# Final sums, norm and output stores of the upper half of the tokens moved beside the last expert of a hybrid attention and expert layer

## The reference

```python
x = x + gt1 * (merged @ lp['w_out'])
h2 = rms_norm(x, lp['norm2_g']) * (1 + sc2) + sh2
x = x + gt2 * hierarchical_moe(h2, ...)      # each token: two of 16 experts, 1024 -> 256 -> 1024
...
hid = jax.nn.silu(jnp.einsum('td,edf->tef', x, w_g)) * jnp.einsum('td,edf->tef', x, w_u)
hid = hid * gate[:, :, None]
y = jnp.einsum('tef,efd->td', hid, w_d)
...
y = rms_norm(x, final_norm_g)
```

## Time and profile before

| | us |
|---|---|
| median of 3 runs | 1568.53 |
| lowest and highest of them | 1565.21 and 2982.1 |
| the profiled execution, its own time | 1567.61 |
| its span, first to last instruction | 1565.7 |

### The profile page before, as it was taken

One profiled execution on the slowest core, in us unless ns is written; L12 is line 12 of the kernel. 1 busy time (PEld: TensorE's weight loads), 2 busy tenths in 40 slices (PEclk: granted clock), 3 DMA queues, 4 the chain that ended last, 5 costly groups with the idle time before them and its releaser, 6 DMA issues.

```text
span 1565.7 us, 21878 instructions
## 1 busy us (share of the span) xinstructions
PE 1476.5 (94%) x8155; PEld 1232.6 (79%) x8155; DVE 1006.5 (64%) x1498; ACT 655.4 (42%) x890; POOL 269.0 (17%) x167
## 2 busy tenths in 40 slices
PE   5999999999999899999999999999999599999990
PEld 4788888777888678888788888888888589888880
DVE  7698433046546477778877764334556888888875
ACT  6312222221123566666566642111332367677753
POOL 0112211123324101001100000000000124444430
PEclk9999999999999999999999999999999699999995
DMA  9345443320001010000000034423524378988858
GB/s 374 136 158 184 160 162 145 109 106 28 28 31 65 34 45 0 0 0 34 12 1 0 15 104 142 150 89 116 184 82 188 111 239 264 259 270 262 254 149 290
DMA packets 52449, 194.81 MB, mean 124 GB/s; under 512 B 9370, under 2 KB 18442, under 8 KB 40992
## 3 DMA queue, kind: packets, MB, share of 16 engines
q1 hardware_dynamic: 42144, 172.31, 30.2%
q0 software_dynamic: 10240, 21.61, 6.9%
HBM read 157.03 MB, written 43.58 MB: 128 GB/s over the span
## 4 chain that ended last, share of the span: by engine, by line
PE 48%; DVE 8%; ACT 3%; DMA 3%; issue 2%; POOL 0%; DVEq 0%; SPq 0%; POOLq 0%; ACTq 0%
PE psum L1636 9%; PE psum L1816 6%; PE psum L1837 5%; PE psum L1592 4%; PE psum L1741 4%; PE psum L1820 3%; PE psum L1578 2%; PE psum L1575 2%; PE psum L1576 2%; PE psum L1752 2%; PE psum L1561 2%; PE psum L1563 2%; PE psum L1562 2%; ACT prob L1902 2%; PE psum L1801 1%
## 5 line engine op out<-in xcount | busy, mean ns | idle before, releaser
L353 PE MATMUL psum<-h_hi,w_hi 128*128 128x512 f32 x720 | 182.9, 362 | 2.1 <-issue 2.1
L353 PE MATMUL psum<-h_lo,w_hi 128*128 128x512 f32 x720 | 179.7, 358 | 0.0
L353 PE MATMUL psum<-h_hi,w_lo 128*128 128x512 f32 x720 | 179.3, 357 | 0.0
L2148 DVE TENSOR_TENSOR pT_lo<-psum,pT_hi 128x512 fp32r<-128x512 f32 x192 | 126.2, 686 | 55.7 <-ACT pT_hi L1908 55.7
L353 PEld LDWEIGHTS psum<-h_hi,w_hi 128*128 128x128 f32 x720 | 119.7, 188 | 28.8 <-issue 8.5
L1908 ACT CAST pT_hi<-psum 128x512 fp32r<-128x512 f32 x192 | 104.6, 589 | 84.4 <-PE psum L1592 84.4
L353 PEld LDWEIGHTS psum<-h_lo,w_hi 128*128 128x128 f32 x720 | 119.4, 188 | 21.7 <-issue 0.5
L353 PEld LDWEIGHTS psum<-h_hi,w_lo 128*128 128x128 f32 x720 | 119.4, 188 | 21.3
L714 POOL TENSOR_TENSOR w_lo<-w_raw,w_hi 128x1024 fp32r<-128x1024 f32 x30 | 76.0, 2533 | 319.9 <-ACT w_hi L555 319.9
L867 DVE SCALAR_TENSOR_TENSOR ada_junk<-adaT,cs_rows 128x1024 f32<-128x1024 f32 x64 | 84.3, 1317 | 65.7 <-DMA adaT<-in_w_adaT 62.5
L1902 ACT ACTIVATE prob<-psum,nmax,q_row 128x1536 f32<-128x1536 f32 x64 | 104.6, 1635 | 31.5 <-DVE nmax L2142 31.5
(11 more groups left out here) (385 smaller groups left out, 2907.8 us busy)
## 6 DMA issues: line engine op xcount, KB each, us to landing
gu_raw<-in_w_gu SPq DMA_DIRECT2D x32, 1024.0 KB, 8.5
w_raw<-in_w_in SPq DMA_DIRECT2D x16, 1024.0 KB, 5.0
adaT<-in_w_adaT SPq DMA_DIRECT2D x16, 1024.0 KB, 6.0
dn_raw<-in_w_dn SPq DMA_DIRECT2D x16, 1024.0 KB, 7.3
gates<-gst SPq DMA_DIRECT2D x14, 640.0 KB, 3.1
xt<-in_x SPq DMA_DIRECT2D x10, 512.0 KB, 8.6
merged<-gates SPq DMA_DIRECT2D x8, 640.0 KB, 4.0
stage<-gates SPq DMA_DIRECT2D x8, 640.0 KB, 3.9
```

The costliest lines, as they stand in the source:

```text
L353: mm = pe.matmul(psum[:, par_sets[j] + g:par_sets[j] + g + w], a[j][:, k, :], b[:, k, g:g + w], start=(k == 0 and a is w_hi and b is h_hi) ...
L2148: nc.vector.tensor_tensor(pT_lo[b][g % 2][:], psum[:, TP + 512 * b:TP + 512 * b + 512], pT_hi[b][g % 2][:], ALU.subtract).then_inc(s[f"a_t ...
```

## The change

- Tiles 5 to 9 (tokens 640 and up, all latent) are loaded from y_sum as soon as the additions of the last expert but one have landed, and they are squared, normed and stored without the last expert's rows.
- The last expert's rows of those tokens are handled by themselves. POOL gathers their sums from y_sum into `late[0]` and `late[1]` (row numbers in `lat_ids`, computed in `slot_table`; the other rows of the slots get numbers out of bounds and are left out). DVE adds the last expert's `yst` rows, ACT and DVE norm them, and POOL scatters them to the output, over what the tile stores left there, when all five tile stores have landed.
- The last expert's accumulating additions now write only tokens below 640. When they have landed, SP loads tiles 0 to 4. The context tiles' gate product and sum stand behind the norm of tiles 5 to 9 and of the late rows on DVE, and the sum goes to `y` instead of `x1`.
- SP's list: load 5 to 9, store 5 and 6, wait for the last additions, load 0 to 4, store 7, 8, 9, 2, 3, 4, 0, 1. `f_all` is gone.
- In the last step, slot 1 of expert 14's down product stands ahead of the second half of `gate_up` of expert 15, and writes to PSUM at `XT_PS` instead of `Y_PS`. Its gate weights on ACT and its `y_out` on DVE are ahead of `dn_high` and `dn_low` of expert 15. The down products of expert 15 go by halves of the hidden dimension: both slots with c = 0, then both with c = 1.
- In the first unit of the short attention ACT copies both halves of the probabilities.
- The branches on `n_spare` of ACT and DVE stand at the very end; their bodies load, norm and store all ten tiles again.

The diff, cut to its core:

```diff
                     nc.scalar.copy(sprobT[z % 2][0][:], psum[:, turned_at(z, 0):turned_at(z, 0) + 512]).then_inc(s["s_out_a"], 1)
+                    if z == 0:
+                        act.wait_ge(s["s_turned"], 2)
+                        nc.scalar.copy(sprobT[0][1][:], psum[:, turned_at(0, 1):turned_at(0, 1) + 512]).then_inc(s["s_out_d"], 1)
...
                 for z in range(SHORTS):
                     if z < SHORTS - 1:
                         short_low(z + 1)
-                    short_turned(z)
+                    if z:
+                        short_turned(z)
...
+        def y_at(e, r):
+
+            if isinstance(e, int) and e == NE - 2 and r:
+                return XT_PS
+            return 0 if last_rows(e, r) else Y_PS
...
-        def total(t):
-
-            return x1[:, t, :] if t < CTX_TILES else y[t][:]
-
-        LOADED = (0, 2, 1, 3) + tuple(range(4, TILES))
-        ENDED = ((2, 4), (0, 2), (4, 7), (7, TILES))
+        LATE = NE - 1
+        late = [at(f"late{r}", [P, D], F32, RHL + (20 + 4 * r) * KB) for r in range(HOME)]
...
+
+        def late_y(r):
+
+            return yst_last if r else yst[0]
+
+        ENDED = ((HALF, 7), (7, TILES), (CTX_TILES, HALF), (0, CTX_TILES))
+        LATE_AT = 2
...
-                sp.wait_ge(s["f_all"], 1)
-                for t in LOADED:
+                sp.wait_ge(s["e_down"], 2 * LATE)
+                for r in range(HOME):
+                    sp.wait_ge(s[f"e_y_st{r}"], 16 * LATE)
+
+                def load_y(t):
                     sp.dma_start(y[t][:], io["y_sum"][t * P:(t + 1) * P, :]).then_inc(landed[t], 16)
+                for t in range(HALF, TILES):
+                    load_y(t)
                 for n, t in enumerate(ended):
+                    if n == ENDED[0][1] - ENDED[0][0]:
+                        for r in range(HOME):
+                            sp.wait_ge(s[f"e_y_st{r}"], 16 * NE)
+                        for u in range(HALF):
+                            load_y(u)
                     sp.wait_ge(s["f_normed"], n + 1)
-                    sp.dma_start(io["y"][t * P:(t + 1) * P, :], total(t)).then_inc(s["f_st"], 16)
-                sp.wait_ge(s["f_st"], 16 * TILES)
+                    sp.dma_start(io["y"][t * P:(t + 1) * P, :], y[t][:]).then_inc(s["f_st" if t < HALF else "f_lat_st"], 16)
+                sp.wait_ge(s["f_lat_st"], 16 * (TILES - HALF))
+                sp.wait_ge(s["f_st"], 16 * HALF)
...
-                add_y(NE - 1, 0)
-                add_y(NE - 1, 1)
+                for r in range(HOME):
+                    pool.wait_ge(s[f"e_y_st{r}"], 16 * LATE)
+                for r in range(HOME):
+                    pass_wait(pool)
+                    nc.gpsimd.indirect_dma_start(late[r][0:T, :], None, io["y_sum"], bass.IndirectOffsetOnAxis(lat_ids[0:T, r:r + 1], 0),
+                                                 bounds_check=TOK - 1, oob_is_err=False).then_inc(s[f"e_xg{r}"], 16)
+                for r in range(HOME):
+                    pool.wait_ge(s["e_y"], HOME * LATE + r + 1)
+                    pass_wait(pool)
+                    nc.gpsimd.indirect_dma_start(io["y_sum"][0:HALF * P, :], bass.IndirectOffsetOnAxis(out_ids[0:T, HOME * LATE + r:HOME * LATE + r + 1], 0), late_y(r)[0:T, :], None,
+                                                 bounds_check=HALF * P - 1, oob_is_err=False, compute_op=ALU.add).then_inc(s[f"e_y_st{r}"], 16)
+                pool.wait_ge(s["f_lat_st"], 16 * (TILES - HALF))
+                pool.wait_ge(s["f_late_normed"], HOME)
+                for r in range(HOME):
+                    pass_wait(pool)
+                    nc.gpsimd.indirect_dma_start(io["y"], bass.IndirectOffsetOnAxis(lat_ids[0:T, r:r + 1], 0), late[r][0:T, :], None,
+                                                 bounds_check=TOK - 1, oob_is_err=False).then_inc(s["e_xg0"], 16)
                 n_left = pool.value_load(n_spare[0:1, 0:1], min_val=0, max_val=SPARE)
-                pool.wait_ge(s["e_y_st0"], 16 * NE)
-                pool.wait_ge(s["e_y_st1"], 16 * (NE - 1))
-                pool.wait_ge(s["e_xg1"], 16 * (NE + 1))
+                pool.wait_ge(s["e_xg0"], 16 * (NE + 1 + HOME))
...
+                def down_half(e, q, r, c):
+                    pe.wait_ge(s["e_hid_hi"], 2 * e + c + 1)
+                    pe.wait_ge(s["e_hid_lo"], 2 * e + c + 1)
+                    o = y_at(e, r)
+                    for n, (x, w) in enumerate(((hid_hi, dn_hi), (hid_hi, dn_lo), (hid_lo, dn_hi))):
+                        for h in range(2):
+                            mm = pe.matmul(psum[0:T, o + 512 * h:o + 512 * (h + 1)], x[q][:, c, r * T:(r + 1) * T], w[q][:, c, 512 * h:512 * (h + 1)],
+                                           start=(n == 0 and c == 0), stop=(n == 2 and c == 1))
+                    return mm
...
-                    o = Y_PS if more(e, 1) else (Y_PS, 0)[r]
-                    if later(e, 1) and o:
-                        pe.wait_ge(s["e_y"], 2 * e + r)
-                    elif r and o:
-                        pe.wait_ge(s["e_y"], 1)
+                    if y_at(e, r) == Y_PS:
+                        if later(e, 1):
+                            pe.wait_ge(s["e_y"], 2 * e + r)
+                        elif r:
+                            pe.wait_ge(s["e_y"], 1)
...
+                def last_down(e, q):
+                    pe.wait_ge(s["e_dn_hi"], e + 1)
+                    pe.wait_ge(s["e_dn_lo"], e + 1)
+                    pe.wait_ge(s["e_y"], 2 * e - 1)
+                    for c in range(2):
+                        for r in range(2):
+                            mm = down_half(e, q, r, c)
+                            if c:
+                                mm.then_inc(s["e_down"], 1)
 
                 def step(e, q):
                     if later(e, 2) and more(e, 1):
...
                         down(e - 1, 1 - q, 0)
                     if more(e, 1):
                         turn(e + 1, 1)
+                    else:
+                        down(e - 1, 1 - q, 1)
                     gate_up(e, q, 1)
-                    if later(e, 1):
+                    if later(e, 1) and more(e, 1):
                         down(e - 1, 1 - q, 1)
...
-                down(NE - 1, 1, 0)
-                down(NE - 1, 1, 1)
+                last_down(NE - 1, 1)
...
+                    if not more(e, 1):
+                        gate_weights(e - 1, 1)
                     dn_high(e, q)
-                    if later(e, 1):
+                    if later(e, 1) and more(e, 1):
...
-                if_spare(act, body)
...
                 nc.scalar.activation(rt[:, 0:1], eps[:], ACT.Sqrt)
 
+                def square(m, rows, acc, n=P):
+                    if m >= 2:
+                        act.wait_ge(s["f_sq"], m - 1)
+                    nc.scalar.activation(junk[m % 2][0:n, :], rows, ACT.Square, accum_out=acc).then_inc(s["f_sq"], 1)
+
+                def late_roots():
+                    m = squares(LATE_AT) - HOME
+                    for r in range(HOME):
+                        act.wait_ge(s["f_late_added"], r + 1)
+                        square(m + r, late[r][0:T, :], late_sq[0:T, r:r + 1], T)
+                    act.wait_ge(s["f_sq"], m + HOME)
+                    nc.scalar.activation(late_rt[0:T, :], late_sq[0:T, :], ACT.Sqrt, bias=eps[0:T, :], scale=1.0 / D).then_inc(s["f_rt"], 1)
+
                 for n, (a, b) in enumerate(ENDED):
+                    if n == LATE_AT:
+                        late_roots()
                     for u in range(a, b):
                         if u < CTX_TILES:
-                            act.wait_ge(s["f_summed"], u + 1)
+                            act.wait_ge(s["f_summed"], CTX_TILES)
                         else:
                             act.wait_ge(landed[u], Y_IN[u])
-                        m = ended.index(u)
-                        if m >= 2:
-                            act.wait_ge(s["f_sq"], m - 1)
-                        nc.scalar.activation(junk[m % 2][:], total(u), ACT.Square, accum_out=ssq[:, u:u + 1]).then_inc(s["f_sq"], 1)
-                    act.wait_ge(s["f_sq"], ended.index(b - 1) + 1)
+                        square(squares(n) + u - a, y[u][:], ssq[:, u:u + 1])
+                    act.wait_ge(s["f_sq"], squares(n) + b - a)
                     nc.scalar.activation(rstd[:, a:b], ssq[:, a:b], ACT.Sqrt, bias=eps[:], scale=1.0 / D).then_inc(s["f_rt"], 1)
+                if_spare(act, body)
...
+                    own.step(ts(lat_off[0:T, :], id_sum[0:T, HOME * LATE:HOMES], HALF * P + 0.5, 4096.0, ALU.is_lt, ALU.mult))
+                    own.step(nc.vector.scalar_tensor_tensor(lat_ids[0:T, :], lat_off[0:T, :], -1.0, id_sum[0:T, HOME * LATE:HOMES], ALU.add, ALU.add))
...
                     if more(e, 1):
                         gu_low(e + 1, 1 - q, 1)
                     else:
+                        y_out(e - 1, 1)
                         dn_low(e, q)
                     hidden(e, 1)
```

(48 more changed lines are left out.)

58 lines of the change are left out of this document (34 added, 24 removed).

## The result

| | before | after |
|---|---|---|
| median of 10 runs, us | 1567.64 (1565.21 to 2982.1) | 1570.5 (1568.66 to 1572.08) |
| ratio after to before | | 1.0021, 95% interval [1.0012, 1.0029] |
| profiled execution: its own time, its span | 1567.61, 1565.7 | 1571.26, 1569.4 |

The account below looks back on a forecast made before the run. DVE and DMA were taken to bound the last 21 us, behind a 12.87 us DVE gap. DVE's end at 1560.3 plus 3.45, less 0.8, gave span 1563.0, 2.7 less than before; median 1565.8 us, range 1562 to 1572.

Parts of the forecast that it names:

- + 3.45: End of kernel: storing the last tile and what follows take 3.45 us after DVE's last scaling, as before.
- part 4: DVE's queue from the late sums on: 23.9 us against 21.4 before, DVE ending at 1560.3, span 1563.75.
- rival (b): End of kernel: POOL ends last, second scatter landing at 1561.3, or 1564.8 at worst, giving median 1566.9; chance 0.12.
- part 5: Short attention and `slot_table`: ACT's copy cuts PE's wait, 0.8 us gained; two small instructions cost nothing, at most 0.4.
- the prediction's own signs: Trace after: second scatter lands ahead of SP's last store; prediction wrong if the chain of waits ends on POOL.
- late landings (a): Tail: slow addition and gather landings stall DVE's late sums 4.5 us, median 1570.3, 1.8 slower than before; chance 0.15.
- Part 1: Order on PE in the last step: the last down products end 1.4 us sooner, 1525.2 against 1526.66.
- Part 2: Early tiles' arrival: expert 14's additions land at 1525.9 after 8.5 us; DVE is done with tiles 5 and 6 at 1536.4.
- Part 3: POOL's gathers, issued at 1526.8 and 1528.7, land after 8.7 us at 1535.5 and 1537.4, just hidden from DVE.
- The rule weighed: Skill's claim that DVE with two SBUF inputs spares POOL's descriptor making, scatters issuing in 1.58 us; rejected, 3.1 counted.

Follow-up runs that it names:

- e9: e1 with gathers, late sums, roots, norms and scatters left out, so tiles 5 to 9 lack the last expert's rows; ratio to before 0.9974.
- e8: e1 with POOL's two scatters left out, the late rows computed but not written; ratio to before 0.9997.
- e1: The changed kernel, but SP instead of POOL waits for the landing of POOL's two scatters; ratio to before 1.0001.
- e3: The changed kernel, but SP stores tiles 7, 8 and 9 before waiting for the last additions and loading tiles 0 to 4; ratio to before 1.0029.
- e4: The changed kernel with the edits of e1 and e3 together; ratio to before 1.0024.
- e6: The kernel before with only the last step's new order of down products, gate weights and y_out; ratio to before 1.0007.
- e5: The kernel before with only the short attention's part: ACT copies both halves of the probabilities in the first unit; ratio to before 0.9995.
- e2: The kernel before, but POOL waits for all ten output stores before its block ends; ratio to before 1.0032.

## Why the prediction was wrong

The tail grew from 54.2 to 59.3 us, 5.1. In steps, each the difference of two kernels:

| step | tail, us | ratio |
|---|---|---|
| overlap of tiles 5 to 9, and the order (before to e9) | -3.0 | 1 to 0.9974 |
| gathers, late sums, norms (e9 to e8) | +4.1 | to 0.9997 |
| scatters (e8 to e1) | +2.1 | to 1.0001 |
| POOL's wait and drain at the very end (e1 to after) | +1.8 | to 1.0021 |

The first two steps are resolved by their ratios (0.9974 and 0.9997 have intervals apart); the third is not. The last is 1.8 us in two profiled executions and 3.1 by the ratios; e1 shows where the 1.2 between them lies.

The same 5.1 us by place, from the two traces alone: DVE ends 0.7 us sooner in the tail, SP comes to its exit 5.9 us behind DVE in place of 3.2 (2.7 more), and the end comes 3.3 us behind SP's exit in place of 0.2 (3.1 more). So even with the drain hidden this tail would be 2.0 us longer than before.

**The step that failed** is the "+ 3.45" at the end of part 4, "The store of the last tile and what follows it take 3.45 us" taken over from before, together with rival (b), "2.4 ahead of SP's end". In place of 3.45 us there were 9.3. Three terms were off. Times of parts 1 to 4 have part 5's 0.8 us still in them; where they are set beside the trace below, it is taken off.

- **What follows POOL's last DMA** was taken as nothing. It is a drain of 5.61 us. Every version has one, of 5.3 to 5.6 us where POOL's DMAs have landed: hidden before, last in after. It doesn't stand in the page, which doesn't count such instructions. A landing at 1563.3 was enough for POOL to end 3.1 us after SP (1566.04 to 1569.13). Two of the prediction's own signs miss it: the second scatter did land ahead of SP's last store (1563.31, 1565.80), and the chain of waits ends on DVE.
- **The store of tile 9** was given at most 5.4 us, from the earlier trace rows. It took 10.4, behind the five loads of tiles 0 to 4, a company that no store had before; in e3 and e4, where it goes ahead of these loads, it took 3.2. POOL stood until 1554.3, and issued at 1555.22 and 1556.69 in place of 1549.1 and 1552.5.
- **The last store** takes 5.7 us from issue (1560.09) to landing, where before it took 3.0. In the four kernels without scatters beside it, it took 3.6. So in the 3.45 stood a landing that the change itself made longer.

The landing of the scatters, 1563.3, was 2.8 later than the working's 1560.5 (1561.3 less 0.8) and under its worst of 1564.0, and still the kernel was slower: rival (b) had the right mechanism, POOL last, and a false point of decision. From the landing (1563.3) to the end of the span (1569.4) are 6.1 us. So "the second scatter must land after 1566.5" had to read after 1560.4 (1566.5 - 6.1), and the working's own landing, 1561.3, lies behind that: its sum with the drain in it would have been slower than before by 0.9 us. That the median of 1570.5 fell inside the range was luck: the range reached that far for late landings (a), which did not come.

**The other steps.**

- Part 1: 1.4 us forecast for the last products, 1.24 measured. By itself it brought nothing that e6 can tell.
- Part 2: loads forecast at 1525.4, issued at 1523.47. The addition of expert 14's slot 1 was issued 1.2 sooner (1515.31 for 1516.5) and landed after 8.09 us rather than 8.5. It didn't wait for POOL, as the part has it: slot 0's addition took 1.58 us there and not 3.10, and POOL then waited for DVE. DVE was done with tiles 5 and 6 at 1534.66, 1535.6 forecast.
- Part 3: the gathers landed 8.6 and 9.5 us after issue, 8.7 taken; DVE's sum began at 1534.58 and POOL wasn't waited for. Rival (a), late landings, didn't happen there.
- Part 4, DVE's queue: 1534.66 to 1560.06 is 25.4 us, 23.9 forecast. 1.84 of it is a pause ahead of the root of tiles 7 to 9: tile 9 landed 11.9 us after its issue, beside gathers and additions, where the first tile was given 4.1 and each further one 1.2. The text named a pause of over 1 us as a sign against it, and by that sign it was partly wrong; DVE still ended only 0.6 later than the 1559.5 forecast, since it had started early.
- The last additions were issued at 1527.12 and 1529.05 and landed at 1540.3, 1539.2 forecast, but by 11.3 us from an earlier issue and not by 7.5 from a later one: two misses that nearly cancel, which is luck. DVE didn't wait for tile 0, as said.
- Part 5: 1.1 us are won at the place (PE resumes 2.90 us after the turn began before, 1.81 after), 0.6 of it is left at the next barrier, 0.8 was forecast. e5's 0.9995 agrees, and would agree with nothing too.
- The rule weighed: additions beside a DVE subtraction of two SBUF tiles took 2.74 us again, those with DVE idle 1.62 and 1.59, but the scatters took 1.17 us beside a scaling (1555.22) and 1.00 beside the small instructions of a root (1556.69), not the 3.1 taken. In e3 and e4 the second scatter ran beside a product of two SBUF tiles (L2715, L2716) and took 1.42 and 1.72 us, the first 1.03. So the lengthening isn't of additions alone; it shows beside TENSOR_TENSOR on two SBUF tiles, and hardly beside the scaling, which reads two SBUF tiles too. The Trainium skill, "SBUF — State Buffer", section "Who interferes with whom", infers that the making of descriptors is spared: the scatters of after agree with it, the additions beside subtractions and the second scatters of e3 and e4 don't. From the first issue to the end of the second the scatters took 2.5 us where the working had 6.5; the 4 us saved went into tile 9's store, which landed at 1554.2, 6.0 later than the working's 1548.2.

Two things stay open: what GpSimd's drain does, and how much of the change's ratio (3.3 us) against its tail (5.1 us) is the short attention and how much the spread of single executions, since the runs of this kernel lie 3.4 us apart.

## What to carry to other kernels

When an engine's last work is moved to the end of a kernel, its exit moves too: look in the single records for what each engine does after its last instruction, and put it behind the new end. Where the engine still has DMAs in flight, let another one wait for them: here that was worth 3 us (e1). Work pulled forward into a gap wins what the next limit leaves, here 3.0 us of tail since the second half still waited for the same additions, and the separate handling of 108 rows gave back 4.1. A landing time belongs to the company in which it was measured (ten stores took 2.9 to 5.4 us before, and one behind five loads 10.4, ahead of them 3.2), so list what will be in the queues before you take a row as a bound.

## What was not expected of the hardware

- GpSimd's drain at the end of the last block, the one in which it issues indirect DMAs, took 5.29 us in five kernels and 5.45 to 5.61 in three, with all of its DMAs landed, in e2 30 us before; at other places in these kernels it took 0.03 to 1.40 us. With DMAs in flight it took 9.2, 9.5 and 11.4 us (e1, e4, e9) and ended 2.8, 2.8 and 2.7 us after their landing.
- An accumulating indirect DMA of 108 rows of 4 KB took 6.5 to 11.5 us to land in before; with part of the rows left out, beside loads and gathers, 11.3 and 11.7 in after. The scatters of part of such rows took 4.8 and 6.6 us in after, 6.1 to 6.8 in e3 and e4.
- The issue of an indirect DMA on POOL varied from 1.00 to 3.10 us with what DVE did beside it and with the kind of DMA.
